# Seven half-block products in place of eight for the three output projections of a two-block recurrent network

## What is computed

```
# mixer 1 (attention + mLSTM), latent and context tokens
y_lat, y_ctx = concat([ya, yb]) @ w_out_ab[0]        # (512 | 256, 2048) @ (2048, 1024)
x = x + gate * y_lat;  ctx = ctx + gate_c * y_ctx
# mixer 2 (gated linear attention), latent tokens only
x = x + gate * ((rms(o) * silu(z)) @ w_out_c[0])     # (512, 2048) @ (2048, 1024)
# mixer 3 (RG-LRU + delta net), latent tokens only
x = x + (g_rnn * y_rnn + g_dn * y_dn) @ w_out_2      # (512, 1024) @ (1024, 1024)
h = rms(x) ...                                       # after each of them: the next norm
```

## Time and profile before

| | |
|---|---|
| median of 3 runs | 3827.97 us (3821.84 to 3830.68) |
| profiled execution | 3824.72 us, of it 3822.9 us span from first to last instruction |
| matmul busy (PE) | 3695.1 us, 97% of the span |
| VectorE (DVE) busy | 1693.9 us, 44% |
| ScalarE (ACT) busy | 1281.6 us, 34% |
| GpSimd (POOL) busy | 873.4 us, 23% |
| granted TensorE clock, mean | 0.989 of full |

### The profile page before, as it was taken

The page is one execution under the profiler, slowest core; times in us unless marked ns, Lnnn a source line. Parts: engine busy times, 40 slices in busy tenths (PEclk is TensorE's granted clock), DMA queues, the critical chain, the costliest instruction groups (busy, mean ns, idle before and its releaser), DMA issues.

```text
span 3822.9 us, 52391 instructions
## 1 busy us (share of the span) xinstructions
PE 3695.1 (97%) x21802; PEld 2260.1 (59%) x21802; DVE 1693.9 (44%) x3047; ACT 1281.6 (34%) x2379; POOL 873.4 (23%) x888
## 2 busy tenths in 40 slices
PE   7999999999999999999999999999999999999998
PEld 3565555655555545666667764444455554458887
DVE  1433432233322010777777772254577751034543
ACT  3434443222222011444444451476454431010000
POOL 0000000101100000666666662023344530000000
PEclk9999999999999999999999999999999999999999
DMA  5111002010102111111111011121101111222221
GB/s 214 50 64 72 31 23 88 23 66 1 66 33 88 44 61 66 46 45 45 45 45 45 29 64 42 58 87 62 68 18 46 43 44 59 99 88 85 84 75 55
DMA packets 24253, 226.53 MB, mean 59 GB/s; under 512 B 2641, under 2 KB 5201, under 8 KB 8785
## 3 DMA queue, kind: packets, MB, share of 16 engines
q1 hardware_dynamic: 24016, 223.18, 15.6%
HBM read 221.07 MB, written 2.10 MB: 58 GB/s over the span
## 4 chain that ended last, share of the span: by engine, by line
PE 91%; DVE 4%; ACT 1%; DMA 1%; issue 1%; POOL 1%; DVEq 0%; SPq 0%; POOLq 0%; ACTq 0%
PE bank L1218 9%; PE bank L1549 7%; PE bank L1165 6%; PE bank L1228 5%; PE bank L979 4%; PE bank L1076 4%; PE bank L932 4%; PE bank L1576 3%; PE bank L1341 3%; PE bank L1208 3%; PE bank L918 3%; PE bank L1101 2%; PE bank L998 2%; PE bank L1300 2%; PE bank L1132 2%; PE bank L1480 2%
## 5 line engine op out<-in xcount | busy, mean ns | idle before, releaser
L1218 PE MATMUL bank<-hT,ring 128*128 128x256 f32 (+1 forms) x1024 | 349.8, 490 | 0.0
L1218 PEld LDWEIGHTS bank<-hT,ring 128*128 128x128 f32 x1024 | 189.6, 190 | 122.0 <-issue 108.1
L1165 PE MATMUL bank<-Y,ring 128*128 128x512 f32 (+1 forms) x704 | 248.8, 516 | 0.0
L1165 PEld LDWEIGHTS bank<-Y,ring 128*128 128x128 f32 x704 | 134.3, 191 | 114.4 <-issue 107.7
L979 PE MATMUL bank<-hT,ring 128*128 128x256 f32 (+1 forms) x512 | 186.2, 500 | 2.4 <-ACT hT L1653 2.4
L1341 PE MATMUL bank<-hT,ring 128*128 128x512 f32 x384 | 178.9, 600 | 4.7 <-ACT Y L1659 4.7
L932 PE MATMUL bank<-hT,ring 128*128 128x256 f32 (+1 forms) x512 | 182.3, 493 | 0.0
L1228 PE MATMUL bank<-ring,hT 128*128 128x128 f32 x1536 | 182.0, 277 | 0.0
L1228 PEld LDWEIGHTS bank<-ring,hT 128*128 128x128 f32 x1536 | 176.3, 192 | 2.1
L1076 PE MATMUL bank<-hT,ring 128*128 128x256 f32 (+1 forms) x512 | 171.8, 486 | 0.0
L1637 ACT ACTIVATE arena<-xT 128x512 f32<-128x512 f32 (+1 forms) x40 | 23.5, 587 | 409.1 <-DVE xT L2376 239.3
(11 more groups left out here) (464 smaller groups left out, 7369.9 us busy)
## 6 DMA issues: line engine op xcount, KB each, us to landing
ring<-in_w SPq DMA_DIRECT2D x60, 2048.0 KB, 7.8
ring<-in_w SPq DMA_DIRECT2D x17, 1536.0 KB, 7.0
ring<-in_w SPq DMA_DIRECT2D x20, 1280.0 KB, 5.4
ring<-in_w SPq DMA_DIRECT2D x12, 1024.0 KB, 4.8
ring<-in_w SPq DMA_DIRECT2D x8, 1408.0 KB, 5.9
ring<-in_w SPq DMA_DIRECT2D x19, 512.0 KB, 3.4
xT<-in_xT SPq DMA_DIRECT2D x1, 3072.0 KB, 11.7
out<-hT SPq DMA_DIRECT2D x8, 256.0 KB, 2.1
```

The lines of the kernel that those rows point to most:

```text
L1165: ins = e.matmul(m[:, 0:b - a], w[:, k, sl(j % 2)], src[:, k, a:b], start=k == 0, stop=k == kt - 1)
L1218: ins = e.matmul(m[:, 0:b - a], w[:, k, sl(1 + d)], hT[:, k, a:b], start=k == 0, stop=k == 7)
```

## The change

Each pair of output tiles (2p, 2p+1) of the three projections is now made by seven products over half the input tiles and half the columns. With w = half the columns (256, or 128 for the context), product n writes bank 0, 1, 3, 2, 0, 3, 2 for n = 0 to 6: products 0 and 4 go into bank 0 and need no combination of inputs, products 1, 2, 3 need sums of weight blocks (S1, S2, S0) and differences of activation halves (T1, T2, T0), product 5 needs T3, product 6 needs S3. A new step `sv_begin` makes all differences and the first pair's sums in VectorE; it begins behind the wait for the last tile of what is multiplied. For the first pair of a stage the products are in the order 0, 4, 1, 2, 3, 5, 6. Tiles 0 and 1 of `oc` stay as they were. The norm steps are now issued by pairs (`norm_pairs`) as before `down`. The rest of the program is the same.

```diff
+def norm_pairs(n, name, begun=()):
+    parts, made = range(NORM_PARTS[n]), []
     for p in range(4):
+        made += [("nx", n, s, j) for j in (2 * p - 2, 2 * p - 1) if j > 0 for s in parts]
+        made += list(begun) if begun and not p else [(name, p)]
+        made += [("nq", n, s, j) for s in parts for j in (2 * p, 2 * p + 1)]
+    return made + [("nx", n, s, 6) for s in parts] + [("nm", n, i, s) for i in range(2) for s in parts]
...
-         + [("tables",)] + norm_tiles(1, "oab") + norm_rest(1) + [("zc", j) for j in range(15)]
+         + [("tables",)] + [("sv_begin", "oab")] + norm_pairs(1, "oab") + norm_rest(1) + [("zc", j) for j in range(15)]
...
+         + norm_pairs(2, "oc7", [("oc", 0), ("oc", 1), ("sv_begin", "oc")])
...
+         + [("tables",)] + [("sv_begin", "wo")] + norm_pairs(3, "wo") + norm_rest(3) + gate_up_steps()
...
+            def seven(name, p):                                  # TensorE
...
+                    for n in (0, 4, 1, 2, 3, 5, 6) if begin else range(7):
...
+                        if n in (1, 2, 3, 6):
+                            q.wait_ge(*on("sv_s", (name, p, {1: 1, 2: 2, 3: 0, 6: 3}[n])))
+                        if n in (1, 2, 3, 5):
+                            q.wait_ge(*on("sv_t", (name, s, {1: 1, 2: 2, 3: 0, 5: 3}[n], sv_parts(name)[-1])))
+                        if n == 4:
+                            q.wait_ge(*on("sv_p1", (name, p, s)))
+                        if n in (5, 6):
+                            q.wait_ge(*on("sv_u", (name, p, s, n - 4)))
...
+            def seven(name, p):                                  # ScalarE: the copy of product 0
...
+                    e.activation(sv_tmp[r % 2][1][:, 0:w], bank[spot[name, p, s, 0]][:, 0:w],
+                                 ACT.Copy).then_inc(up("sv_p1", (name, p, s)), 1)
...
+            def sv_begin(name):                                  # VectorE
...
+                if name == "oab":
+                    q.wait_ge(*on("na_y", (7, 1)))
+                    q.wait_ge(*on("ml_out", (3, 1, 1)))
+                elif name == "oc7":
+                    q.wait_ge(*on("gl_out", 15))
+                else:
+                    q.wait_ge(*on("mixed", 7))
+                for n in (0, 1):
+                    sv_sums(name, p, n)
+                for n in range(4):
+                    sv_halves(name, 0, n)
+                    if n > 1:
+                        sv_sums(name, p, n)
+                if name == "oab":
+                    for n in range(4):
+                        sv_halves(name, 1, n)
```

More of the change, by code:

```diff
@@ L1170, in oab @@
[L1170 to L1178, removed]
+            def seven(name, p):
+                if name != "wo" or p % 2 == 0:
+                    slab("oc" if name == "oc7" else name, 2 * SEVEN[name][0])
+                spot["sv_slab", name, p] = open_w["oc" if name == "oc7" else name][1]
+                (m, segs), (g_lo, g_hi, u_lo, u_hi) = SEVEN[name], sv_factors(name, p)
+                begin = p == (1 if name == "oc7" else 0)
+                for s, (a, b) in enumerate(segs):
+                    w, t = (b - a) // 2, 4 * ((p * len(segs) + s) % 2)
+                    o = [take(t + n, (name, p, s, n), ("sv_u", (name, p, s, i)))[:, 0:w] for n, i in enumerate((3, 0, 5, 4))]
+                    lo, hi = (lambda h, k: sv_half(name, s, h, k, k + 1)[:, 0, :]), (lambda h, k: sv_half(name, s, h, m + k, m + k + 1)[:, 0, :])
+                    for n in (0, 4, 1, 2, 3, 5, 6) if begin else range(7):
+                        i, left, first = ((0, g_lo, True), (1, sv_sum(name, 1), True), (3, sv_sum(name, 2), True),
+                                          (2, sv_sum(name, 0), True), (0, g_hi, False), (3, u_hi, False), (2, sv_sum(name, 3), False))[n]
+                        if n in (1, 2, 3, 6):
[6 more added lines that the diff above has]
+                            q.wait_ge(*on("sv_u", (name, p, s, n - 4)))
+                        for k in range(m):
+                            if name == "oab" and p == 0 and n == 0 and k == 0:
+                                q.wait_ge(*on("na_y", (7, 1)))
+                            if name == "oab" and p == 0 and n == 4 and k in (0, 6):
+                                q.wait_ge(*on("ml_out", (3 if k else 2, s if k else 1, 1)))
+                            if name == "wo" and p == 0 and n in (0, 4):
+                                q.wait_ge(*on("mixed", k + n))
+                            right = (lo(0, k), sv_t(name, s, 1, k, k + 1)[:, 0, :], sv_t(name, s, 2, k, k + 1)[:, 0, :],
+                                     sv_t(name, s, 0, k, k + 1)[:, 0, :], hi(0, k), sv_t(name, s, 3, k, k + 1)[:, 0, :], hi(1, k))[n]
+                            ins = e.matmul(o[i], left[:, k], right, start=first and k == 0, stop=k == m - 1,
+                                           skip_group_check=True)
+                        ins.then_inc(up("sv_mm", (name, p, s, n)), 1)
+                if name != "wo" or p % 2:
+                    give("oc" if name == "oc7" else name, "sv_mm", (name, p, s, 6))
@@ L1180, in oc_, with oab, oc7, wo @@
+            def oab(p):
+                seven("oab", p)
+            def oc7(p):
+                seven("oc7", p)
+            def wo(p):
+                if p == 0:
+                    proj.cells[:] = [0, 1, 2, 3]
+                    proj.at = -1
+                seven("wo", p)
             def oc_(j, c):
@@ L1501, in mixd @@
                 give("mixd", "mix_dp_mm", j)
[L1503 to L1515, removed]
             def gu(j):
@@ L2385, in oc, with oab, oc7, wo @@
+            def oab(p):
+                if p == 0:
+                    q.wait_ge(*on("ada_added", (0, 5)))
+                seven("oab", p)
+            def oc7(p):
+                seven("oc7", p)
+            def wo(p):
+                seven("wo", p)
             def oc(j):
```

162 lines of the change are left out of this document (117 added, 45 removed).

## The result

The changed kernel takes 3804.26 us (median of 4 runs, 3802.43 to 3805.69), the kernel before 3824.9 us beside it; the ratio is 0.9944, 95% interval 0.9927 to 0.9961. The forecast was 3806 us in a range from 3797 to 3819.

What follows compares the result with a forecast made beforehand. TensorE, busy 97% of the span, was taken as the bound. Matmuls saved 34.8 us, less 8.5 at starts and 4.4 at ends, gave 21.9: 3802.8 from the profiled 3824.72, predicted as a 3806 us median, range 3797 to 3819.

Steps and rivals of the forecast that it cites:

- Matmuls, 34.8 us: TensorE time saved by seven products: 18.3 us in `oab`, 9.9 in `oc`, 6.6 in `wo`.
- The load rival: Narrow context products of `oab` are paced by 192 ns weight loads: 36 us more, about 3842 us; chance 4%.
- the rule: Skill's 45% surcharge for 128-column matmuls: `oab`'s 448 context records would take 22 us more, cancelling the gain.
- Start of `oab`, 4.55 us: TensorE waits in `oab`'s first pair: 0.7 for ScalarE's copy, 1.75 for T1, 2.1 ahead of product 5.
- product 4 directly follows product 0: In each stage's first pair, product 4 waits 0.7 us for ScalarE's copy of product 0.
- The 2.1: At `oab`'s start, product 5 waits 2.1 us for the second combination, behind VectorE's context differences.
- `oc` and `wo`: Matmul gains 9.9 and 6.6 us, less start waits of 1.15 and 2.8 and 1.05 at each end.
- The middle at nothing: After a stage's first pair, VectorE's work fits under the matmuls, so later pairs cost no waits.
- that rival: VectorE's order makes a wait in every pair, 15 groups: 3821 us at 1 us each; chance 8%.
- The ends, 2.3 + 1.05 + 1.05: Norm roots begin later after the last matmul: 2.3 us in `oab`, 1.05 each in `oc` and `wo`.
- The clock: Rival: the clock falls in the new start waits, 3.3 us once or 10 in all three, 3809 to 3816; chance 16%.
- the forecast's own sign: Prediction wrong if narrow records take over 0.12 us, waits recur in pairs 1 to 3, or the clock drops inside a stage.

Runs made afterwards that it cites:

- e11: Changed kernel with `oab`'s context half by eight products, in the next pair's other two banks, each taken at first use: 3808.54 us, 0.9957 of the kernel before.
- e1: Kernel before with only `oab` changed to seven products, `oc` and `wo` as before: 3817.78 us, ratio 0.9974 to the kernel before.
- e4: The changed kernel timed again, unaltered, on the chip of the single-stage runs: 3804.05 us, ratio 0.9937 to the kernel before.
- e6: Changed kernel with tile 6's running sum made before tile 7's last addition in all three stages: 3805.02 us, ratio 0.9942 to the kernel before.
- e7: Changed kernel with `oab`'s context half by eight products, in the banks with which the next pair begins: 3814.87 us, ratio 0.9967 to the kernel before.
- e9: The changed kernel timed once more, unaltered, as base for the kernels beside it on one chip: 3803.49 us, ratio 0.994 to the kernel before.
- e10: Changed kernel with banks taken at first use, early first weight sums (`oab`, `wo`) and later context differences; timed beside the changed kernel: 3798.4 us, 0.9926 of the kernel before.
- e5: Changed kernel with banks taken at first use, early first weight sums (`oab`, `wo`) and later context differences; first timing: 3800.71 us, 0.9934 of the kernel before.

## Why the prediction held, step by step

- **Matmuls, 34.8 us.** Right. The long piece of 768 records from 1252.48 holds three latent halves at the old pace; the other 432 records come to (121.04 - 336 x 0.2158) / 432 = 0.1123 us against the 0.1117 taken.
- **The load rival and the rule.** Fell. The Trainium skill ("TensorE: Matmul & The Clock Gate", "Back-to-back issue gap") has 128-column matmuls at 81 ns where the isolated formula gives 56, 45% more; the trace has 0.5% over the pace of the kernel before. e11 shows it by difference too.
- **Start of `oab`, 4.55 us.** The sum is right, its parts are not. From first matmul to last end the stage takes 152.1 us; the forecast's own terms (146.7, 1.0 of clock, 4.55) give 152.25. Inside it product 0 is slowed by 2.6 and not 1.0, the wait for T1 is hidden by that, product 5 stands 1.15 (not 2.1), and the copy is waited for twice (0.64 and 0.52 between matmuls). The sum held because VectorE's chain sets the start of product 5, and that chain was sized rightly: 19.5 us from its first weight sum to product 5, some 19.7 in the forecast. A step that was wrong is the copy's: "product 4 directly follows product 0" was applied to the latent half alone, though the context half has the same order. The 2.1 was too large because the clock delayed the products while VectorE went on; with the clock up (e1) the wait before product 5 was 1.8 and that for T1 1.5, near the terms.
- **Missed: the wait for banks**, 1.0 us ahead of product 0 (0.8 to 1.3 in the six profiles with this start: after, e1, e4, e6, e7, e9), gone in e10 and e11. The forecast has no wait there; the code asks for all four banks at once. By e7 and e11 it costs nothing by itself, since VectorE's chain decides when product 1 can begin: without it the waits behind product 0 are longer by as much.
- **`oc` and `wo`.** Net 7.7 and 2.75 forecast, 7.63 and 2.81 measured. In `wo` T1 is waited for 1.6 of the 1.85, and T2 with its sum is 0.3 late where 0.25 was forecast; in `oc` the wait for T1 is 0.2 of the 0.45.
- **The middle at nothing.** Right: all waits of L1221 lie in first pairs, so that rival fell.
- **The ends, 2.3 + 1.05 + 1.05.** Right at full clock: 4.45 us to `oab`'s root in e10 and e5 (4.5 forecast), 3.7 in the others (3.6). In the profile after, the low clock adds 1.0 to `oab`'s.
- **The clock.** The rival had it fall inside the new waits. It fell ahead of them, before `oab`'s product 0 began, and slowed that product by 2.6 us, and it fell at `oab`'s end, and it did not fall after `wo`, which gave 2.8 back. By the forecast's own sign, a clock that drops inside a stage, this step is wrong, though the low clock at `oab`'s start added nothing to the stage. "Everything between the stages of equal length" failed: `oab`'s first matmul comes 7.7 us later in the profile after, 6.7 of them from code that is the same in both kernels, and over the profiles it begins between 1213.7 and 1223.4. The 3.25 us added between profile and median are of that size.

All together: stages 10.8 + 7.6 + 2.8 = 21.3 us shorter, less 1.0 for banks (the lengths begin at product 0), plus 2.8 after `wo`: 23.1 from one pair of profiles, with the drift elsewhere 19.0 in the span, 20.6 to 24.1 in the three pairs of medians. The forecast 21.9 lies among them, partly by errors that cancel and partly by luck with the clock, which it had at nothing outside the new waits. The mean granted clock is 0.9903 over the fourteen executions of the changed kernel and 0.9891 over the forty of the kernel before in the three groups; by that up to 4.6 us of the gain, the 2.8 after `wo` included, came from a higher clock (an estimate, 0.0012 x 3815).

## What to carry to other kernels

A stage bound by TensorE gains from seven products in place of eight what the pace per column says, down to 128 columns, as long as the operands come from an engine that is half idle; what remains to be paid lies in its first pair and its last. At a stage's start, find the chain that decides when the first late product can begin; here it was VectorE's, so a wait for banks and a slow first product cost nothing behind it. Shorten that chain: make weight sums early, though not in front of what the mixer itself still waits for, and put behind the first combinations whatever only a later half needs. An operation moved forward to shorten a tail must not stand in front of the last combination; and when a tail shrinks, compare the first tile after it before counting the gain.

## What the runs showed of the hardware, unexpected

- Low-clock stretches (1.2 GHz, half of full) of one and the same code differ between executions in place, number and length: 11 to 15 of them in a span, most of 3.4 to 10.2 us, with 29 to 41 us of clock missing in all. A difference of a few us between two profiles is read from the stages, not from spans.
- A longer way from the last matmul to the root went with fewer falls: behind `wo`, 3 of 3 profiles with 2.6 us from last matmul to root fell, 2 of 11 with 3.5 to 3.7. Why is open.
- VectorE's subtraction of 2048 float32 elements took 2.28 to 2.29 us, the estimate from two smaller sizes having been 2.28.
